# Cached value pages multiplied in four groups of four instead of eight groups of two

## What is computed

```python
for each of 8 sequences:                       # moba_sample
    k_past = cache_k[pages].reshape(256, 8, 128)   # two pages of this sequence
    v_past = cache_v[pages].reshape(256, 8, 128)
    logits = q . [k_past | k_new] + bias            # the past block, and the new tokens (causal)
    p = softmax(logits)
    out = p_past @ v_past + p_new @ v_new           # p_past @ v_past: two products per head, one per page
hp = hp + (out * silu(gate)) @ moba_w_out
```

## Time and profile before

| | |
|---|---|
| median of 3 runs | 507.18 us (506.43 to 507.96) |
| the profiled execution, its own time | 506.81 us |
| its span, first to last instruction | 504.8 us |
| mean granted clock of TensorE | 0.997 |
| TensorE matmul / weight load busy | 491.4 us (97%) / 424.8 us (84%) |
| VectorE / ScalarE / GpSimd busy | 359.9 us / 259.3 us / 96.6 us |
| DMA | 125.54 MB, 249 GB/s mean |

### The profile page before, as it was taken

One profiled execution on the slowest core, in us unless ns is written; L12 is line 12 of the kernel. 1 busy time (PEld: TensorE's weight loads), 2 busy tenths in 40 slices (PEclk: granted clock), 3 DMA queues, 4 the chain that ended last, 5 costly groups with the idle time before them and its releaser, 6 DMA issues.

```text
span 504.8 us, 9913 instructions
## 1 busy us (share of the span) xinstructions
PE 491.4 (97%) x3689; PEld 424.8 (84%) x3689; DVE 359.9 (71%) x637; ACT 259.3 (51%) x532; POOL 96.6 (19%) x139
## 2 busy tenths in 40 slices
PE   7999999999999999999999999998798999999997
PEld 5989978899779977899899999976566778999885
DVE  3955539884799829894599978978766755776662
ACT  6735532574428633365553546835435655655630
POOL 0291004520072101820000152463002000000000
PEclk9999999999999999999999999999899999999999
DMA  9993969999799997999937979989987557684211
GB/s 265 350 348 104 275 244 319 382 354 241 274 342 387 242 268 277 367 322 227 265 113 270 343 223 258 207 206 215 237 295 229 200 185 244 225 310 145 84 52 52
DMA packets 86770, 125.54 MB, mean 249 GB/s; under 512 B 5491, under 2 KB 51524, under 8 KB 86596
## 3 DMA queue, kind: packets, MB, share of 16 engines
q1 hardware_dynamic: 85874, 124.63, 81.1%
q0 software_dynamic: 768, 0.28, 0.4%
q10 hardware_dynamic: 82, 0.02, 0.0%
HBM read 98.93 MB, written 27.57 MB: 251 GB/s over the span
## 4 chain that ended last, share of the span: by engine, by line
PE 92%; DVE 4%; DMA 1%; issue 1%; ACT 1%; SPq 0%; DVEq 0%; ACTq 0%
PE bank L928 46%; PE bank L925 19%; PE bank L909 7%; PE bank L1037 3%; PE bank L1099 2%; PE bank L1157 2%; PE bank L1051 1%; PE bank L984 1%; PE bank L1203 1%; DMA st<-in_x_prompt 1%; DVE w_lo L1565 1%; PE bank L1017 1%; PE bank L1018 1%; PE bank L1019 1%; PE bank L1005 1%
## 5 line engine op out<-in xcount | busy, mean ns | idle before, releaser
L1565 DVE TENSOR_TENSOR w_lo<-w_raw,w_hi 128x512 fp32r<-128x512 f32 x207 | 144.2, 735 | 61.8 <-ACT w_hi L1227 61.2
L1227 ACT ACTIVATE w_hi<-w_raw 128x512 fp32r<-128x512 f32 x208 | 118.8, 620 | 60.7 <-PE bank L928 35.0
L928 PE MATMUL bank<-xn_hi,w_hi 128*128 128x320 f32 x320 | 100.2, 317 | 0.8 <-ACT w_hi L1227 0.7
L928 PE MATMUL bank<-xn_hi,w_lo 128*128 128x320 f32 x320 | 97.8, 310 | 0.1
L928 PE MATMUL bank<-xn_lo,w_hi 128*128 128x320 f32 x320 | 97.7, 309 | 0.0
L925 PE MATMUL bank<-w_hi,xn_hi 128*128 128x512 f32 x160 | 64.5, 403 | 0.0
L928 PEld LDWEIGHTS bank<-xn_hi,w_hi 128*128 128x128 f32 x320 | 59.7, 188 | 5.0 <-issue 2.8
L925 PE MATMUL bank<-w_lo,xn_hi 128*128 128x512 f32 x160 | 62.5, 391 | 0.0
L925 PE MATMUL bank<-w_hi,xn_lo 128*128 128x512 f32 x160 | 62.4, 390 | 0.0
L928 PE MATMUL bank<-ym_hi,w_hi 128*128 128x320 f32 x192 | 61.0, 317 | 0.0
L928 PEld LDWEIGHTS bank<-xn_lo,w_hi 128*128 128x128 f32 x320 | 59.8, 188 | 0.4 <-DVE xn_lo L1614 0.2
(11 more groups left out here) (290 smaller groups left out, 784.6 us busy)
## 6 DMA issues: line engine op xcount, KB each, us to landing
w_raw<-in_ret_w_in SPq DMA_DIRECT2D x23, 1024.0 KB, 10.9
st<-in_state_ret SPq DMA_DIRECT2D x32, 512.0 KB, 8.6
out_ret_state_sample<-st SPq DMA_DIRECT2D x32, 512.0 KB, 4.7
w_raw<-in_ret_w_out SPq DMA_DIRECT2D x8, 1024.0 KB, 8.6
w_raw<-in_moba_w_in SPq DMA_DIRECT2D x8, 1024.0 KB, 6.6
w_raw<-in_w_kv SPq DMA_DIRECT2D x8, 1024.0 KB, 8.6
cache<-in_cache_v SPq DMA_DIRECT2D x16, 512.0 KB, 5.3
cache<-in_cache_k SPq DMA_DIRECT2D x48, 128.0 KB, 6.7
```

The lines of the kernel that those rows point to most:

```text
L928: mm = pe.matmul(bank[out][:, 0:T], w[:, wk, P * tile:P * tile + P], x[:, k, :], **flags)
L1227: act.activation(w_hi[:, c % 2, part], w_raw[:, c % RAW, part], ACT.Copy).then_inc(w_hi_done, 1)
L1565: dve.tensor_tensor(w_lo[:, c % 2, part], w_raw[:, c % RAW, part], w_hi[:, c % 2, part].bitcast(F32), ALU.subtract).then_inc(w_lo_done, 1)
```

## The change

The 16 PV steps move. Before, they stand in pairs at half tiles 6, 9, 12, 15, 21, 24, 27 and 30. After, they stand in fours at half tiles 5, 12, 19 and 26. The loads of the pages move with them in SP's order of work.

```diff
     g = [[] for _ in range(34)]
-    for n, at in enumerate((6, 6, 9, 9, 12, 12, 15, 15, 21, 21, 24, 24, 27, 27, 30, 30)):
+    for n, at in enumerate((5, 5, 5, 5, 12, 12, 12, 12, 19, 19, 19, 19, 26, 26, 26, 26)):
         g[at].append(("PV", n))
```

## The result

The changed kernel is slower. Its median is 511.89 us (509.58 to 516.39, 4 runs) against 506.93 us for the kernel before (506.43 to 507.96, 4 runs, three of them those of the forecast's 507.18): a ratio of 1.0101 [1.006, 1.0142], in brackets the 95% interval. Measured twice more, beside 35 runs of the kernel before each time, it came to 1.0067 [1.0037, 1.0098] and 1.0063 [1.0031, 1.0095], about 3.3 us. The slowdown is clear each time, its size less so: the 5 us of the first comparison rest on four runs that lie 6.8 us apart. The forecast was 507.3 us and no change; the range ended at 509.4.

A forecast was written before the change was run, and what follows sets the result against it. PE was taken to bound the stretch, matmul behind matmul from 389.9 us. Borders -0.8, page 7 wait +0.9, other refills 0, later work 0 gave +0.1 us on 507.18: 507.3 us, no change, range 506.0 to 509.4.

The forecast's parts named there:

- The reading of what bounds PE: From 389.9 us on PE waits once, 0.2 us; only taking PE time away gains, each PE wait lengthens the result.
- Step 1: Borders of PV groups on PE: entering and leaving costs 0.2 us; eight become four, 0.8 us gained.
- Step 2: Loads of value pages 4 to 7 between groups 1 and 2: page 7 lands 418.5, PE waits 0.9 us; far bound 3.0.
- The first rival: All pages in time, page 7 landing before PV_7 needs it: change -0.8, 506.4 us; chance 0.28.
- The rule of the Trainium skill: Prices a transfer at about 2.0 us plus bytes over 436 GB/s; page 7 would land at 415.6, before due.
- Step 3: Page loads ahead of PV groups 3 and 4: no wait; far bound 1.6 us for page 15.
- Step 4: Work behind the moved PV steps (chunk 44, scores, SB, XR): no cost; 0.7 us of slack left at B(1).
- refills late: PE waits at PV_7 and again at PV_15: +1.0 to +4.8 us, middle 2.9 (510.1 us); chance 0.14.
- late scores: VectorE's slack of 0.7 at B(1) is used up, PE waits about 0.5: 507.8 us; chance 0.08.
- The list of what would prove the forecast wrong: Second group without gap (506.4 us), PE waiting for page 15, or at B or XR for VectorE or ScalarE.

The follow-up runs named there:

- The refill-free pair: Without loads of pages 4 to 15: kernel before (507.89 us, stage 80.2) and changed kernel with third group behind B 4 and A 5 (506.24 us, 79.7).
- experiment 3: Kernel before with only the PV pairs of half tiles 21 and 24 moved into one group at 19: 510.37 us, ratio 1.0041.
- third_behind_a5: Changed kernel with the third PV group behind B 4 and A 5 of the same half tile: 510.40 us, ratio 1.0037.
- after_again: Changed kernel, unaltered, measured and profiled again beside the kernel before: 511.40 us, ratio 1.0067.
- xr_later: Changed kernel, third group behind B 4 and A 5, chunks 45 and 48 behind pages 7 and 15, last two XR steps half tile later: 507.83 us.
- chunk45_behind_page7: Changed kernel with SP issuing the load of weight chunk 45 behind page 7 instead of ahead of it: 508.38 us, ratio 1.0015.

## Why the prediction was wrong

**The reading of what bounds PE** held: the waits of PE in this stretch, added to the borders, give the stage within 0.5 us in all 13 profiles of the table.

**Step 1, group borders: right.** -0.8 us forecast. The refill-free pair gives 80.2 against 79.7 + a wait of 0.5 of its own, so 0.8 to 1.0. One reading in it was not quite right: it took 0.505 us for a page from a pair's 1.01 in the chain and foresaw 2.02 for a group of four. In the same view a group takes 1.89 (433.98, above), so 0.13 of the pair's 1.01 belonged to the border.

**Step 2, the refill between groups 1 and 2: right in mechanism, somewhat small.** Forecast: page 7 issued at 408.6, landing at 418.5, a wait of 0.9. After, its issue and landing (answers to the earlier trace rows; on SP's queue page 7 is the first of four):

```profile
409.47 10.97 SPq L718 DMA_DIRECT2D cache<-in_cache_v  x4
```

```profile
cache<-in_cache_v SPq DMA_DIRECT2D x1, 512.0 KB, 9.5
```

It lands at 419.0, and PE waits 1.09. The first of the six transfers was issued 0.45 us later than forecast, the landing came 0.5 later: the rate of 338 GB/s was met here. In three more profiles with this order of SP the wait was 2.05, 1.93 and 1.44, with landings 10.1 to 10.4 us after the issue; the mean of the four, 1.6, is 0.7 above my term and within the far bound of 3.0. So the close hit of the first profile was in part luck. The first rival (all in time) fell. The rule of the Trainium skill that stood behind it (DMA: Bandwidth & Descriptors, "Anatomy of one DMA") would give, as an estimate from the first issue at 404.40, 404.4 + 2.0 + 9.6 = 416.0. That section fits the rule to single transfers issued by GpSimd, which the prediction left out; here SyncE issues six in a row. The trace has 419.0, so the rule is not to be carried over to such a backlog.

**Step 3, the other refills: partly.** Nothing for groups 2 to 3 was right. For page 15 I took nothing and kept 1.6 as far bound; PE waited 1.00 and 1.14 us in two of four profiles and nothing in the other two. It is a term of about half a microsecond on average.

**Step 4, behind the moved steps: the step that failed.** It said of the third group "B(4) and A(5), behind four pages now, gain distance" and of XR "XR waits for PV_12 to PV_14, all done sooner. No cost." Both sentences look only at the nearest reader. The distance from A(4) to B(4) did grow, by the four pages. But A 5 is not only something that PE does: it is what VectorE is waiting for, [0.49 <-PE bank L1191] in the trace of before. Four pages in front of it hold VectorE for two microseconds, and from there VectorE and ScalarE passed the delay on undiminished to XR, where ScalarE's copies were only 0.28 and 0.44 us early. The row of VectorE's wait and these leads were there to be read; I checked A to B for each head and the PV condition of XR, not the order of work of VectorE and ScalarE from A 5 on. Cost: 2.0 us alone (experiment 3).

So the forecast sum was -0.8 + 0.9 + 0 + 0, and the three profiles of the changed kernel give -0.8 + 1.5 (page 7) + 0.3 (page 15) + 1.6 (XR) = +2.6, for stages that were longer by 2.4, 3.4 and 2.8. Of the rivals, "refills late" named the right sign and, by luck, about the right size in total (+2.9): its page waits, 3.7 at the middle, were twice the mean of 1.9 that was measured, and the XR waits, of which it knew nothing, made up for it; the "late scores" looked at B 1, where nothing happened. The list of what would prove the forecast wrong did name a wait for page 15 and a wait at XR for ScalarE; both came, and to the second I had given no price and no case of its own. The chance of 0.13 for slower was too small: one priced term could have been 3 us, and one step on three engines had been costed at nothing on the word of its nearest reader.

## What to carry to other kernels

Before a block of matmuls is moved in front of a step, ask who is idle for that step now. If another engine's idle time just before it ends with PE, a chain of that engine may start there, and what is put in front can go through undiminished to the next place where PE waits for it, as it did here over 31 us; so compare the lead at that place (here 0.28 and 0.44 us) with the length of the block (here 1.95 us). Putting like matmuls side by side gained only the border, 0.2 to 0.25 us each here, while a load that used to have three half tiles must now have its whole group's bytes in the queue ahead of it: put what is not urgent (a weight chunk) behind the last page that is.

## What the runs showed of the hardware

**Two engines that keep each other in step passed a delay on exactly.** From VectorE's A 5 to ScalarE's XR copies took 31.33 to 31.36 us in the nine profiles in which no PV group stands directly behind A 5, with different pages, places and starts. In the five with the third group there it took longer, 31.74 to 31.76 us, and 32.56 in third_behind_a5, where VectorE waited for PE once more behind the late page 15 (0.48 us at line 1713). In the stage of the changed kernel VectorE was busy only 52.0 and ScalarE 46.5 of 82.6 us. Shares of 63% and 56% don't mean that there is slack.

**The scatter between executions lies largely ahead of the stage.** The stage began anywhere from 390.5 to 396.8 us in the profiles, in work that no kernel here alters. One part is a stop of PE ahead of the 32x32 matmuls of line 1099 that waits for nothing that the profile shows: 0.7 us before, 2.1 after, nothing in after_again, and 4.6 in xr_later. PE's timeline there:

```profile
374.37 1.10 PE L1099 MATMUL bank<-scr,wide 32*32 32x256 f32 x15 [4.61 <-issue]
375.40 0.80 PE L925 MATMUL bank<-w_hi,xn_hi 128*128 128x512 f32 x1
...
376.42 0.63 PE L925 MATMUL bank<-w_lo,xn_hi 128*128 128x512 f32 x1
...
379.05 0.39 PE L925 MATMUL bank<-w_hi,xn_hi 128*128 128x512 f32 x1
```

and three stretches (width; busy PE, PEld, DVE, ACT, POOL; clock; DMA share; GB/s):

```profile
360.00:372.00 12.00, 8.85 (x139) 6.30 (x139) 7.38 (x10) 2.70 (x7) 0.00 (x0) 0.85 1.09 268
372.00:384.00 12.00, 9.63 (x76) 6.90 (x77) 5.73 (x9) 4.08 (x10) 0.00 (x0) 0.72 0.51 186
384.00:397.00 13.00, 11.58 (x168) 8.56 (x155) 8.64 (x17) 7.71 (x19) 2.74 (x5) 1.00 0.73 232
```

Here the stop costs twice: the granted clock is 0.72 on average from 372 to 384, a mixture of its levels of 1.2 and 2.4 GHz, and matmuls behind the stop take 0.63 us instead of 0.39 until 378. What PE's sequencer waited for was not tried. The stop is not the whole of the scatter: the stage began at 391.3 both in after_again, without a stop, and in chunk45_behind_page7, with one of 1.8 us. The rest stays open.

**One queue's landings vary by a microsecond.** The same six transfers from the same queue landed 9.5 to 10.4 us after page 7's issue, in six profiles with the changed kernel's order on SP between chunk 44 and page 7. Where a margin is as small as here, one profile of a landing is one draw.
